# Two transformer blocks on one Trainium2 core: one instruction stream per engine in place of five blocks with barriers, and one modulation product moved to other work units

## The chip, the cores and the metric

The kernel runs on one core of one Trainium2 chip. The metric is the device time of one execution in microseconds, the median over several executions. The core has five engines that run on their own and meet only through semaphores: PE (TensorE, matrix products into the eight PSUM banks), DVE (VectorE), ACT (ScalarE), POOL (GpSimd) and SP (SyncE, which here issues all DMA transfers).

## The reference

Two transformer blocks over one sequence of 256 tokens and 2048 channels, in fp32. Block one: RMS norm, a projection `h @ w_in` whose columns feed a dilated window attention and a gated linear attention, the output projection, then `x + (silu(h @ w_gate) * (h @ w_up)) @ w_down` and a final norm. Block two: a vector c gives six rows of 2048 modulation values,

```
mod = c @ w_ada_2 + b_ada_2          # 2048 x 12288: shift, scale, gate, twice
h = rms_norm(x) * (1 + scale1) + shift1
proj = h @ w_in_2                    # retention, RWKV-7 and block attention
x = x + gate1 * (mixed @ w_out_2)
h = rms_norm(x) * (1 + scale2) + shift2
u = conv3(h @ w_ffn_up_2)            # causal, three taps, per channel
x = x + gate2 * ((silu(u_gate) * u_value) @ w_ffn_down_2)
out = rms_norm(x)
```

## The kernel before

**Weights.** Each large matrix comes in loads of 1 MB (`raw_weights`, four places). A load is two units of 128 x 1024. For each unit ACT writes the high part (`split_hi`, L267), DVE the rest (`split_lo`, L274), and PE makes three products (high x high, high x low, low x high), so that fp32r products give fp32 accuracy. There are four places for split units and the splits run `AHEAD = 3` units ahead: while PE multiplies unit n, ACT and DVE split unit n + 3. `load` lets SP issue load l only when the units that were in its place are split; `split_hi` waits for the load to land and for PE to be done with the unit four before. A unit is 24 matmuls of 256 columns (form "T", the result is transposed) or 12 of 512 columns (form "rows").

**Stages, in order:** first mixer (`FirstMixer`), gate and up (`Glu`, 11 turns of 16 units), down (`Down`, 44 tiles of two units), second mixer (`SecondMixer`, 136 units), up with convolution (`stage_conv_glu`, 11 turns of 16 units), down again, final norm. The first three are one block of instructions (`first_block`); the second mixer, the convolution stage, the second `Down` and the final norm are four more. At the end of a block every engine waits for every other one; between the first two POOL also clears the semaphores (L200, `wait_cleared`).

**What happens at each stage's start.** `Down` first splits four tiles of its activations into high and low (L1720, L1755), which it may do only when the stage before has written them all, in program order; PE begins when `pair_free[0]` and the first low tile are there. The second mixer turns its normalized rows on PE (`turn`, L2050, a matmul with a scaled identity): four of sixteen before the first unit, and two beside each of units 0 to 5. The convolution stage has `Norm`: all sixteen turns first (L402), with L413/L423 and a split of four tiles at a time (L284, L297), then the first unit.

**Modulation.** `mod` is made in twelve groups of 1024 columns. For a group SP issues eight loads of 1 MB (`Ada.load`, L480, two places), DVE makes 16 products (`Ada.product`, L495; the first L497) and PE sums over partitions with 8 matmuls of one column (`Ada.sums`, L507, 16 records in the profile). `Ada.load` m makes SP wait until product 2(m-1) is made, and the weight loads behind it wait too: there is one queue. Groups 6 to 8 are made during `Down` and summed by PE at its end (L1704, 24 matmuls, 48 records). Group 9 belongs to the second mixer: loads at weight loads 57 to 64, products at units 112 to 127, sums at unit 131. Units 104 to 135 are the output projection.

**Second mixer's work beside the units.** `side` (PE), `scalar_side` (ACT) and `vector_side` (DVE) hold what each engine does after unit n. For RWKV, DVE has one instruction or a few in each of units 13 to 35: L2781 at 32 feeds PE's head sums (L2118) at 33, L2789 at 35 feeds PE's transposes (L2247) at 36.

Of the kernel before, what the change touches and what calls it, by code (L numbers as in the profile page):

```python
# [21 lines left out]
ds = bass.ds  # L22
# [95 lines left out]
class Kit:  # L118


    def __init__(self, nc, ctx, ins, at):
# [6 lines left out]
        self.norms = self.turns = 0  # L128
# [8 lines left out]
        self.x_splits = self.act_splits = self.ada_groups = 0  # L137
# [8 lines left out]
        self.w_hi, self.w_lo, self.x_hi, self.x_lo, self.a_hi, self.a_lo = (  # L146
            self.sem(n) for n in ("weights_hi", "weights_lo", "x_hi", "x_lo", "act_hi", "act_lo"))
# [7 lines left out]
        self.gated_norm = [self.sem("gated_norm_" + n) for n in ("mean", "rms", "normed", "turned", "out_dve",  # L155
                                                                 "out_act")]
        self.gated_norms = (0, 0, 0)
        self.row_spread, self.row_copied, self.row_copies = self.sem("row_spread"), self.sem("row_copied"), 0
# [3 lines left out]
        self.square_parts = 1  # L162
# [3 lines left out]
        self.n_scaled = self.sem("norm_scaled")  # L166
        self.n_turned = self.sem("norm_turned")
        self.n_out = [self.sem("norm_out_dve"), self.sem("norm_out_act")]
# [4 lines left out]

    def second_half(self):

        at_h = -(-self.nc.sbuf_base // 32) * 32
        self.hT = self.sb("h_T", [P, KT, S])
        self.x_lo_t = self.at_byte("h_lo_T", at_h, [P, KT, S], R32)
# [17 lines left out]
    def clear_sems(self):  # L196

        self.nc.clear_and_free_semaphores(self.first_sems)
        self.first_sems = []
        self.nc.gpsimd.memset(self.stat[:, 61:62], 0.0).then_inc(self.cleared, 1)  # L200
# [77 lines left out]
def split_x_hi(kit, act, norm):  # L278


    for u in range(4):
        if norm:
            norm.out_act(act, u)
        kit.nc.scalar.activation(kit.x_hi_t[:, 4 * u:4 * u + 4, :], kit.hT[:, 4 * u:4 * u + 4, :], ACT.Copy  # L284
                                 ).then_inc(kit.x_hi, 1)


def split_x_lo(kit, dve, base, norm, wait=None):

    for u in range(4):  # L290
        if norm:
            norm.out_dve(dve, u)
    if wait:
        dve.wait_ge(*wait)
    for u in range(4):
        dve.wait_ge(kit.x_hi, base + u + 1)
        kit.nc.vector.tensor_tensor(kit.x_lo_t[:, 4 * u:4 * u + 4, :], kit.hT[:, 4 * u:4 * u + 4, :],  # L297
                                    kit.x_hi_t[:, 4 * u:4 * u + 4, :].bitcast(F32), ALU.subtract
                                    ).then_inc(kit.x_lo, 1)


def multiply_block(kit, pe, form, j, n0, i, use, xbase, mid=None, spans=None):
# [4 lines left out]
    spans = spans or [(q * P, (q + 1) * P) for q in range(4)]  # L307
    xh, xl = kit.x_hi_t, kit.x_lo_t
    pe.wait_ge(kit.pair_free[j], use + 1 + i)
    for u in range(8):  # L310
        n = n0 + u
        s = n % SPLITS
        if xbase is not None and u % 2 == 0:
            pe.wait_ge(kit.x_lo, xbase + u // 2 + 1)
# [34 lines left out]
def rms_scales(kit, dve, r):  # L349


    nc, stat = kit.nc, kit.stat
    parts = stat[:, 0:16].rearrange("p (t b) -> p t b", t=ST)[:, :, 0:kit.square_parts]
# [11 lines left out]
def rms_root(kit, act, r):  # L365

    bring_root(kit, 32)
# [4 lines left out]
class Norm:  # L372
# [3 lines left out]
    def __init__(self, kit, ctx, wcol, bcol=None, modulated=None):  # L376
        self.kit, self.wcol, self.bcol, self.modulated = kit, wcol, bcol, modulated
        self.r, self.turns = kit.norms, kit.turns
        self.diag = kit.sb(f"norm_diag{kit.turns}", [P, ST, P], ctx)
        kit.norms += 1  # L380
        kit.turns += 1

    def scales(self, dve):
        kit = self.kit
        if self.modulated is not None:
            modulation(kit, self.modulated)
        rms_scales(kit, dve, self.r)
        for t in range(ST):
            kit.nc.vector.tensor_scalar(self.diag[:, t, :], kit.c("ident"), kit.stat[:, 20 + t:21 + t], None, ALU.mult
                                        ).then_inc(kit.n_scaled, 1)  # L390

    def root(self, act):
        rms_root(self.kit, act, self.r)

    def turn(self, pe):
        kit = self.kit
        pe.wait_ge(kit.n_scaled, ST * (self.turns + 1))
        for k in range(KT):
            if k >= 4:
                pe.wait_ge(kit.n_out[k % 2], KT // 2 * self.turns + (k - 4) // 2 + 1)  # L400
            for t in range(ST):
                ins = kit.nc.tensor.matmul(kit.ps[:, 4 + k % 4, t * P:(t + 1) * P], lhsT=kit.x[:, t, k * P:(k + 1) * P],  # L402
                                           rhs=self.diag[:, t, :], start=True, stop=True)
            ins.then_inc(kit.n_turned, 1)

    def out_dve(self, dve, u):

        kit = self.kit
        for k in (4 * u, 4 * u + 2):
            dve.wait_ge(kit.n_turned, KT * self.turns + k + 1)  # L410
            src = kit.ps[:, 4 + k % 4, 0:S]
            if self.bcol:
                ins = kit.nc.vector.tensor_scalar(kit.hT[:, k, :], src, self.wcol(k), self.bcol(k), ALU.mult, ALU.add)  # L413
            else:
                ins = kit.nc.vector.tensor_scalar(kit.hT[:, k, :], src, self.wcol(k), None, ALU.mult)
            ins.then_inc(kit.n_out[0], 1)

    def out_act(self, act, u):

        kit = self.kit  # L420
        for k in (4 * u + 1, 4 * u + 3):
            act.wait_ge(kit.n_turned, KT * self.turns + k + 1)
            kit.nc.scalar.activation(kit.hT[:, k, :], kit.ps[:, 4 + k % 4, 0:S], ACT.Identity, scale=self.wcol(k),  # L423
                                     bias=self.bcol(k) if self.bcol else 0.0).then_inc(kit.n_out[1], 1)
        for half in range(2):
            act.wait_ge(kit.n_out[half], KT // 2 * self.turns + 2 * u + 2)


def stage_final_norm(kit, weight, out):


    nc = kit.nc
    r, done = kit.norms, kit.finals
    kit.norms += 1
    kit.finals += 4
    quarters = [(t, slice(half * D // 2, (half + 1) * D // 2)) for t in range(ST) for half in range(2)]
    with nc.Block() as block:  # L437
        @block.vector
        def _(dve):
            rms_scales(kit, dve, r)  # L440
            dve.wait_ge(kit.loaded, kit.loads_done)
            for t, cols in quarters:
# [1154 lines left out]
class Down:  # L1597
# [115 lines left out]
    def scalar(self, act):  # L1713
# [18 lines left out]
        for k in range(4):  # L1732
            tile(k, 0)
# [1521 lines left out]
```

## Time and profile before

| | us |
|---|---|
| median of 3 executions | 2583.23 |
| their range | 2580.23 to 2594.74 |
| profiled execution, its own time | 2582.93 |
| its span, first to last instruction | 2581.0 |
| PE busy | 2505.3 (97%) |
| DVE busy | 1636.0 (63%) |
| ACT busy | 1144.3 (44%) |

The span is what the rows below divide up; 1.9 us of the execution's own time lie outside it. Times within the trace are counted from the first instruction. "PEclk" is the TensorE clock that was granted in a stretch: 1.00 is 2.4 GHz, 0.5 is 1.2 GHz, and a value between is a mixture of the two in time. A busy PE is not yet PE at full speed.

### The profile page before, as it was taken

To read this page: it belongs to the slowest core of one execution; us is meant where nothing else is said; L and a number is where in the kernel's file an instruction comes from. 1 tells how busy PE (TensorE), PEld (TensorE's weight loads), DVE (VectorE), ACT (ScalarE), POOL (GpSimd) and SP (SyncE) were. 2 spreads that over 40 slices of the span, in tenths; PEclk is the share of its full clock that TensorE was granted. 3 is DMA by queue.
4 is the path that set the end of the run, shared out by engine and by line. 5 is a ranking of instruction groups with operands and counts; after the bars stand their busy time and mean duration, and the time that the engine had idled before them with its cause. 6 is when DMAs were issued, how large, how long until landed. Compare 5 with 4: busy or idle time off the path is not lost. (4 is left out here: it accounts for less than half of the span.)

```text
span 2581.0 us, 41890 instructions
## 1 busy us (share of the span) xinstructions
PE 2505.3 (97%) x17370; PEld 2273.9 (88%) x17370; DVE 1636.0 (63%) x1912; ACT 1144.3 (44%) x1477; POOL 0.3 (0%) x5
## 2 busy tenths in 40 slices
PE   8999999999999999999899999987999999989997
PEld 8888778999999997888898999875999999988886
DVE  4566548777767756777665465556688666654455
ACT  5454344534334334444654333433544444544443
POOL 0000000000000000000000000000000000000000
PEclk9999999999999999999899999998999999999998
DMA  7454457778778767887455334545677555555552
GB/s 268 158 165 157 138 184 273 270 263 292 254 283 279 263 218 261 295 292 273 148 193 162 101 118 130 167 162 212 245 279 276 194 191 190 192 189 184 182 192 98
DMA packets 213832, 541.26 MB, mean 210 GB/s; under 512 B 9050, under 2 KB 14756, under 8 KB 201668
## 3 DMA queue, kind: packets, MB, share of 16 engines
q1 hardware_dynamic: 213700, 539.37, 60.2%
q8 instruction: 99, 1.62, 0.3%
q14 instruction: 33, 0.27, 0.0%
HBM read 534.06 MB, written 5.28 MB: 209 GB/s over the span
## 5 line engine op out<-in xcount | busy, mean ns | idle before, releaser
L274 DVE TENSOR_TENSOR weights_lo<-raw_weights,weights_hi 128x1024 fp32r<-128x1024 f32 x794 | 968.0, 1224 | 830.2 <-ACT weights_hi L267 827.7
L267 ACT ACTIVATE weights_hi<-raw_weights 128x1024 fp32r<-128x1024 f32 x794 | 838.9, 1061 | 1279.0 <-PE ps L334 493.3
L495 DVE SCALAR_TENSOR_TENSOR ada_acc<-ada_w,col,ada_acc 128x1024 f32<-128x1024 f32 x180 | 230.2, 1279 | 2.2 <-DMA ada_w<-in_w_ada_dram 2.1
L334 PE MATMUL ps<-h_hi,weights_hi 128*128 128x256 f32 x1408 | 218.9, 277 | 1.4 <-issue 1.4
L334 PE MATMUL ps<-h_lo_T,weights_hi 128*128 128x256 f32 x1408 | 217.9, 277 | 0.0
L334 PE MATMUL ps<-h_hi,weights_lo 128*128 128x256 f32 x1408 | 217.9, 277 | 0.0
L334 PE MATMUL ps<-glu_x_hi,weights_hi 128*128 128x256 f32 x1280 | 202.8, 280 | 0.0
L334 PE MATMUL ps<-glu_x_lo,weights_hi 128*128 128x256 f32 x1280 | 202.7, 280 | 0.0
L334 PE MATMUL ps<-glu_x_hi,weights_lo 128*128 128x256 f32 x1280 | 202.4, 279 | 0.0
L334 PEld LDWEIGHTS ps<-h_hi,weights_hi 128*128 128x128 f32 x1408 | 186.8, 188 | 2.5 <-issue 2.5
L334 PEld LDWEIGHTS ps<-h_hi,weights_lo 128*128 128x128 f32 x1408 | 186.7, 188 | 0.0
L334 PEld LDWEIGHTS ps<-h_lo_T,weights_hi 128*128 128x128 f32 x1408 | 186.6, 188 | 0.0
L334 PEld LDWEIGHTS ps<-glu_x_hi,weights_hi 128*128 128x128 f32 x1280 | 173.2, 188 | 0.0
L334 PEld LDWEIGHTS ps<-glu_x_lo,weights_hi 128*128 128x128 f32 x1280 | 173.1, 188 | 0.0
L334 PEld LDWEIGHTS ps<-glu_x_hi,weights_lo 128*128 128x128 f32 x1280 | 172.9, 187 | 0.0
L1691 PE MATMUL ps<-weights_hi,h_hi 128*128 128x512 f32 x352 | 112.0, 400 | 7.0 <-DVE h_lo_T L1755 7.0
L1691 PE MATMUL ps<-weights_hi,glu_x_hi 128*128 128x512 f32 x352 | 111.2, 397 | 3.5 <-DVE glu_x_lo L1755 3.5
L1691 PE MATMUL ps<-weights_hi,h_lo_T 128*128 128x512 f32 x352 | 111.6, 398 | 0.0
L1691 PE MATMUL ps<-weights_lo,h_hi 128*128 128x512 f32 x352 | 111.5, 398 | 0.0
L1691 PE MATMUL ps<-weights_hi,glu_x_lo 128*128 128x512 f32 x352 | 111.4, 398 | 0.0
L1691 PE MATMUL ps<-weights_lo,glu_x_hi 128*128 128x512 f32 x352 | 111.2, 397 | 0.0
L1820 PE MATMUL ps<-m_x_hi,weights_hi 128*128 128x256 f32 (+1 forms) x576 | 95.9, 288 | 0.0
(438 smaller groups left out, 3559.4 us busy)
## 6 DMA issues: line engine op xcount, KB each, us to landing
raw_weights<-in_w_in_dram SPq DMA_DIRECT2D x101, 1024.0 KB, 5.2
ada_w<-in_w_ada_dram SPq DMA_DIRECT2D x96, 1024.0 KB, 7.2
raw_weights<-in_w_ffn_up_dram SPq DMA_DIRECT2D x88, 1024.0 KB, 5.2
raw_weights<-in_w_gate_dram SPq DMA_DIRECT2D x44, 1024.0 KB, 5.2
raw_weights<-in_w_up_dram SPq DMA_DIRECT2D x44, 1024.0 KB, 5.3
raw_weights<-in_w_down_dram SPq DMA_DIRECT2D x44, 1024.0 KB, 4.9
raw_weights<-in_w_ffn_down_dram SPq DMA_DIRECT2D x44, 1024.0 KB, 4.8
raw_weights<-in_w_out_dram SPq DMA_DIRECT2D x32, 1024.0 KB, 7.2
```

The source lines that it names most:

```text
L267: kit.nc.scalar.activation(kit.w_hi_t[:, n % SPLITS, :], raw, ACT.Copy).then_inc(kit.w_hi, 1)
L274: kit.nc.vector.tensor_tensor(kit.w_lo_t[:, n % SPLITS, :], raw, kit.w_hi_t[:, n % SPLITS, :].bitcast(F32), ALU.subtract).then_inc(kit.w_l ...
L334: ins = nc.tensor.matmul(out, lhsT=lhsT, rhs=rhs, start=start and m == 0, stop=(k == KT - 1 and m == 2), skip_group_check=True)
L495: step = nc.vector.scalar_tensor_tensor(acc, w, c, acc, ALU.mult, ALU.add)
L1691: ins = nc.tensor.matmul(kit.ps[:, 4 * t + 2 * half + q, :], lhsT=lhsT, rhs=rhs, start=(k == 0 and m == 0), stop=(k + past == w_tiles - 1 ...
L1820: ins = nc.tensor.matmul(out, lhsT=lhsT, rhs=rhs, start=start and m == 0, stop=ends and m == 2, skip_group_check=True)
```

## The change

It rewrites how the stages are put together:

1. All stages are in one block: each engine has one stream from first to last stage. POOL clears the first stages' semaphores while `Down` runs. Semaphores take the place of the barriers: the second mixer's DVE waits for `square_sums >= 8`, SP for `x_weighted >= 4`, the convolution stage for the mixer's `x_squares`, the final norm for `square_sums_2 >= 4`. The table of the square root is brought to ACT before the last squares (`bring_root`) and no longer by `rms_root`.
2. `Down`'s first four tiles are split by the stage before it: `first_hi` and `first_lo` stand in the last turn of `Glu` (after its 16 splits) and of the convolution stage (before the last taps), into places of their own. PE begins with token half 1 (banks 4 to 7) of each half of the columns, and waits for `pair_free` only before token half 0.
3. `ConvGlu` takes the place of `stage_conv_glu` and `Norm`: the class `Turned`, which is the second mixer's way of turning, for both; so four turns before unit 0 and two beside each of units 0 to 5.
4. Group 9 moves: loads at weight loads 11 to 18 (after `s_x2out`), products at units 15 to 37, sums and copy at unit 45 (bank 7). Groups 6 to 8 are summed by PE beside unit 3 of the second mixer, and no longer at the end of `Down`.
5. Smaller moves: the convolution stage's bias row is loaded before its first weights, its products stand at odd units, `Down` waits for `ada_sum` in both places.

```diff
 class Down:
     def tensor(self, pe):
...
-                for t in range(ST):
-                    h, l = (x[:, k % R, t * P:(t + 1) * P] for x in (kit.x_hi_t, kit.x_lo_t))
+                for t in ((1, 0) if begun else range(ST)):
+                    if begun and t == 0:
+                        pe.wait_ge(kit.pair_free[half], self.pairs[half] + 1)
+                    h, l = (x[k % R][:, t * P:(t + 1) * P] for x in (self.hi, self.lo))
...
-        if self.accs:
-            pe.wait_ge(kit.ada_acc, 16 * (self.lead + len(self.accs)))
-            pe.wait_ge(self.s_square, 1)
+    def ada_sums(self, pe):
...
+    def first_hi(self, act):
+        for k in range(4):
+            self.kit.nc.scalar.activation(self.hi[k], self.act_tile(k, 0), ACT.Copy).then_inc(self.kit.a_hi, 1)
+    def first_lo(self, dve):
+        for k in range(4):
+            self.lo_tile(dve, k, 0)
 class Glu:
     def scalar(self, act):
...
+            if half is None:
+                self.down.first_hi(act)
     def vector(self, dve):
...
+            if half is None:
+                self.down.first_lo(dve)
             dve.wait_ge(kit.weights_used, first + 16 + 16 * i)
 class SecondMixer:
+    ADA = (15, 16, 18, 19, 21, 22, 23, 24, 26, 27, 29, 30, 32, 34, 36, 37)
...
-        ada_loads = (57, 58, 59, 60, 61, 62, 63, 64)
+        ada_loads = (11, 12, 13, 14, 15, 16, 17, 18)
...
-                    sp.wait_ge(kit.weights_used, self.first + self.at["out00"].start)
+                    sp.wait_ge(self.s_x2out, 16)
...
+        if n == 3:
+            self.down.ada_sums(pe)
...
-        if n == 131:
-            self.ada.sums(pe, self.lead + 1, 0)
+        if n == self.RET - 1:
+            pe.wait_ge(self.s_ev, 8)
+            self.ada.sums(pe, self.lead + 1, 0, 7)
...
-        s, at = n - 112, None
-        if 0 <= s < 16:
-            self.ada.product(dve, self.lead, 0, s)
+        if n in self.ADA:
+            self.ada.product(dve, self.lead, 0, self.ADA.index(n))
 class ConvGlu:
     def tensor(self, pe):
...
+                for k in range(4):
+                    self.turned.turn(pe, k)
+                for j in range(2):
...
+                        multiply_part(kit, pe, part, first + 8 * j + u, u, self.x_hi, self.x_lo)
+                        if j == 0 and u < 6:
+                            self.turned.turn(pe, 2 * u + 4)
+                            self.turned.turn(pe, 2 * u + 5)
...
+                if isinstance(i, int) and i == self.turns - 1 and j == 1:
+                    self.down.first_lo(dve)
                 for tap in (1, 0):
```

## Rows read from the trace of the kernel before

**Rows 1.** The page: engines' busy time, one product group, one kind of DMA issue

```profile
PE 2505.3 (97%) x17370; PEld 2273.9 (88%) x17370; DVE 1636.0 (63%) x1912; ACT 1144.3 (44%) x1477; POOL 0.3 (0%) x5
...
L495 DVE SCALAR_TENSOR_TENSOR ada_acc<-ada_w,col,ada_acc 128x1024 f32<-128x1024 f32 x180 | 230.2, 1279 | 2.2 <-DMA ada_w<-in_w_ada_dram 2.1
...
raw_weights<-in_w_out_dram SPq DMA_DIRECT2D x32, 1024.0 KB, 7.2
```

**Rows 2.** Waits from 1690 to 1850: who for whom, total us, times, longest

```profile
ACT weights_hi L267 <- DMA raw_weights<-in_w_out_dram: 56.0, 6, 10.4
...
PE ps L1820 <- DVE weights_lo L274: 19.0, 5, 4.6
...
SPq L480 <- DVE ada_acc L495: 78.5, 6, 25.4
```

**Rows 3.** Windows: stretch, its us, busy us (x instructions) by engine, PEclk, DMA share, GB/s

```profile
979.00:987.00 8.00, 4.45 (x13) 3.49 (x13) 5.11 (x7) 2.29 (x5) 0.00 (x0) 0.79 0.22 58
1000.00:1050.00 50.00, 50.00 (x216) 40.26 (x216) 36.09 (x38) 21.63 (x27) 0.00 (x0) 1.00 0.80 292
1230.90:1248.00 17.10, 9.72 (x48) 9.66 (x48) 12.79 (x18) 9.56 (x18) 0.10 (x1) 0.65 0.06 14
1248.00:1274.30 26.30, 26.30 (x208) 26.12 (x209) 16.91 (x30) 16.29 (x28) 0.00 (x0) 0.90 0.54 177
1307.00:1377.00 70.00, 70.00 (x612) 68.73 (x611) 46.69 (x56) 38.10 (x50) 0.00 (x0) 1.00 0.55 172
1342.00:1370.00 28.00, 28.00 (x238) 27.04 (x238) 21.79 (x25) 11.37 (x14) 0.00 (x0) 1.00 0.62 195
1719.92:1785.00 65.08, 44.01 (x147) 33.71 (x147) 39.30 (x34) 16.58 (x21) 0.00 (x0) 0.82 0.62 222
1804.20:1822.50 18.30, 10.27 (x65) 9.88 (x64) 9.17 (x19) 10.65 (x19) 0.00 (x0) 0.81 0.46 173
2308.30:2321.60 13.30, 6.25 (x17) 4.80 (x16) 7.25 (x15) 4.72 (x10) 0.00 (x0) 0.62 0.46 174
```

**Rows 4.** Timeline of DVE before each `Down`: start, us, instruction

```profile
977.37 1.23 DVE L274 TENSOR_TENSOR weights_lo<-raw_weights,weights_hi 128x1024 fp32r<-128x1024 f32 x1 [1.60 <-ACT weights_hi L267]
...
2312.95 0.06 DVE L3105 MEMSET stat<- 128x1 f32 x1
```

**Rows 5.** Timeline where the two norms before a turn begin, and a sum of one group

```profile
1243.74 0.19 ACT L1746 ACTIVATION_READ_ACCUMULATOR y_squares<-x_weighted 128x1 f32 x1
...
1246.14 0.16 DVE L2654 TENSOR_REDUCE stat<-stat 128x4 f32<-128x8 f32 x1 [3.40 <-POOL stat L200]
...
1808.06 0.19 ACT L2637 ACTIVATION_READ_ACCUMULATOR m_squares<-x_rows 128x1 f32 x1
...
1810.88 10.29 PE L402 MATMUL ps<-norm_diag,x_rows 128*128 128x128 f32 x64 [6.67 <-DVE norm_diag L389]
...
565.70 1.84 PE L507 MATMUL ps<-cst,ada_acc 128*128 128x1 f32 x16
```

**Rows 6.** Timeline of DVE and PE in units 27 to 36 of the second mixer

```profile
1345.11 1.23 DVE L274 TENSOR_TENSOR weights_lo<-raw_weights,weights_hi 128x1024 fp32r<-128x1024 f32 x1 [1.50 <-ACT weights_hi L267]
...
1359.92 1.14 DVE L2781 TENSOR_SCALAR rw_gp<-rw_gp,col 128x256 f32<-128x256 f32 x4
...
1368.59 1.23 DVE L274 TENSOR_TENSOR weights_lo<-raw_weights,weights_hi 128x1024 fp32r<-128x1024 f32 x1 [2.09 <-ACT weights_hi L267]
1369.73 1.22 DVE L2789 TENSOR_TENSOR rw_bonus<-ps,rw_v 128x1024 f32<-128x1024 f32 x1
...
1362.80 1.88 PE L2118 MATMUL ps<-rw_gp,cst 128*128 128x512 f32 x4
...
1373.67 0.60 PE L2247 MATMUL ps<-cst,rw_bet 128*128 128x128 f32 x4
```

**Rows 7.** Windows in the convolution stage, before and after its first row sums

```profile
1850.00:1900.00 50.00, 50.00 (x427) 50.00 (x427) 41.31 (x50) 24.64 (x28) 0.00 (x0) 1.00 0.74 267
1950.00:2000.00 50.00, 50.00 (x443) 50.00 (x442) 41.40 (x50) 24.01 (x28) 0.00 (x0) 1.00 0.79 293
```

More of the change, by code:

```diff
@@ L127, in __init__ @@
         self.loads_done = 0
-        self.norms = self.turns = 0
+        self.norms = self.turned = 0
         self.dve_steps = 0
@@ L275, in split_lo, with multiply_block @@
                                 ALU.subtract).then_inc(kit.w_lo, 1)
[L278 to L302, printed above, removed]
+def multiply_block(kit, pe, x, form, j, n0, i, use, mid=None):
     nc = kit.nc
-    spans = spans or [(q * P, (q + 1) * P) for q in range(4)]
-    xh, xl = kit.x_hi_t, kit.x_lo_t
+    spans = [(q * P, (q + 1) * P) for q in range(4)]
+    xh, xl = x
     pe.wait_ge(kit.pair_free[j], use + 1 + i)
@@ L365, in rms_root @@
 def rms_root(kit, act, r):
-    bring_root(kit, 32)
     act.wait_ge(kit.n_mean, r + 1)
     kit.nc.scalar.activation(kit.stat[:, 18:20], kit.stat[:, 18:20], ACT.Sqrt).then_inc(kit.n_rms, 1)
[L372 to L387, printed above, removed]
-        for t in range(ST):
[L389 to L426, printed above, removed]
@@ L1728, in body @@
                 tile(k + 4, i)
-        if self.after:
-            act.wait_ge(kit.weights_used, first)
-            act.wait_ge(kit.pair_free[1], self.pairs[1] + 1)
-        for k in range(4):
-            tile(k, 0)
         self.in_turns(act, body)
@@ new lines, in row_sums, with sync, body @@
+    def row_sums(self, pe, g):
+        kit, nc = self.kit, self.kit.nc
+        pe.wait_ge(kit.ada_acc, 16 * (self.lead + g + 1))
+        for b in range(2):
+            step = nc.tensor.matmul(kit.ps[:, 4 + 2 * g + b, :], lhsT=kit.c("ones"),
+                                    rhs=self.ada.acc[:, b * UN:(b + 1) * UN], start=True, stop=True)
+        step.then_inc(kit.ada_sum, 1)
+    def sync(self, sp):
+        kit, first, lead = self.kit, self.first, self.lead
+        sp.dma_start(self.gate[:, :], kit.ins["b_ada_2"][:, 2 * UN * lead:2 * UN * (lead + 2)].partition_broadcast(P)
+                     ).then_inc(self.s_gate, 16)
+        def body(i):
+            for m in range(8):
+                if m < 4 or not (isinstance(i, int) and i == self.turns - 1):
+                    col = (0, F2 + UN)[m // 4] + UN * i
+                    load(kit, sp, first // 2 + 4 + m, i, block_src(self.w, m % 4, col))
+                if isinstance(i, int) and i < 4 and m % 2:
+                    if i == 0 and m == 1:
+                        sp.wait_ge(kit.weights_used, first)
+                    self.ada.load(sp, lead + i // 2, 0, 4 * (i % 2) + m // 2)
+        load_block(kit, sp, first // 2, 0, self.w, F2)
+        self.in_turns(sp, body)
+        self.head_next(sp, first // 2 + 8 * self.turns)
@@ new lines, in tensor, with body @@
+    def tensor(self, pe):
+        kit, first, uses = self.kit, self.first, self.uses
+        def body(i):
+            if isinstance(i, int) and i == 0:
+                for k in range(4):
+                    self.turned.turn(pe, k)
+                for j in range(2):
+                    part = Part("T", None, 0, j, 8, ())
+                    pe.wait_ge(kit.pair_free[j], uses[j] + 1)
+                    for u in range(8):
+                        if j == 0:
+                            pe.wait_ge(kit.s_xlo, self.turned.before + 2 * u + 2)
+                        pe.wait_ge(kit.w_lo, first + 8 * j + u + 1)
+                        multiply_part(kit, pe, part, first + 8 * j + u, u, self.x_hi, self.x_lo)
+                        if j == 0 and u < 6:
+                            self.turned.turn(pe, 2 * u + 4)
+                            self.turned.turn(pe, 2 * u + 5)
+                return
+            for j in range(2):
+                mid = None
+                if j == 0 and self.summed(i) is not None:
+                    mid = lambda: self.row_sums(pe, self.summed(i))
+                multiply_block(kit, pe, (self.x_hi, self.x_lo), "T", j, first + 8 * j, i, uses[j], mid)
+        self.in_turns(pe, body)
@@ L3225, in program @@
[L3225 to L3231 removed]
+        base = -(-nc.sbuf_base // 32) * 32
+        t = lambda name, off, shape, dt=F32: kit.at_byte(name, base + off * 1024, shape, dt)
+        tiles = lambda name, off: [t(f"{name}{n}", off + n, [P, S], R32)[:, :] for n in range(4)]
@@ new lines, in wide_head, with head, second_head @@
+        def wide_head(w):
+            def head(sp, l):
+                for k in range(LOADS):
+                    load(kit, sp, l + k, 0, wide_src(w, P * k))
+            return head
+        glu = Glu(kit, first, ada, actT[:, :, :], silu[:, :], ins["w_gate"][0], ins["w_up"][0],
+                  wide_head(ins["w_down"][0]))
+        def second_head(sp, l):
+            for u in range(LOADS):
+                load(kit, sp, l + u, 0, block_src(ins["w_in_2"][0], u, SecondMixer.LOW))
+        lo = [t(f"down_lo{n}", a, [P, S], R32)[:, :] for n, a in enumerate((104, 105, 110, 111))]
```

645 lines of the change are left out of this document (300 added, 345 removed).

## The prediction

> **What bounds the kernel now.** I read the page first: PE is busy for 97% of the span, DVE for 63%, ACT for 44% [rows 1]. So only time in which PE stands still, or runs at the lower clock level, can be won, and any PE work that moves from a gap into a busy stretch costs its full length. I then took windows of 50 us over the whole span to find where PE isn't full or PEclk is under 1.00: the start, the seam from `Glu` to `Down`, the seam into the second mixer, the output projection, the seam into the convolution stage, the seam into the second `Down`, and the end. The list of waits names the reasons, and narrow windows price them [rows 2, 3]. The reader should see in each window both the idle time (length less PE busy) and the clock: a gap of 3.55 us at 979 is followed by 1.2 GHz in part of the stretch, so it costs more than its length.
>
> **The output projection holds the largest loss.** From 1719.92 to 1785.00 PE is busy for 44.01 of 65.08 us, at PEclk 0.82 [rows 3]. A matmul of 512 columns takes 50/216 = 0.2315 us at full clock by the `Down` window [rows 3]; spaced by its starts it is 0.233. Of the 147 matmuls 143 are of the projection, worth 33.4 us, and four small ones 0.7. So 34.1 us of work took 65.1: 21.1 us idle and 9.9 us of slowing, together 31.0. Behind it is one chain: SP stood before `Ada.load` for products of group 9, 78.5 us in six waits, the weight loads behind it were issued late, ACT waited 56.0 us for them, DVE for ACT, and PE 19.0 us for DVE [rows 2]; the remaining 2.0 us idle are an attention step behind the same ACT wait.
>
> **The change part by part**, as differences for the path of PE.
>
> *(a) Group 9 leaves the projection: -31.0.* No load there waits for a product any more. What is late next? The projection's 1 MB per two units is 1 MB in 5.6 us, which the DMA engines do easily (292 GB/s in `Down` [rows 3]), and DVE is free for a third of that stretch already with the products in it. I take all of 31.0; the lower bound is 21.1, the idle time alone, if the clock fell for another reason.
>
> *(b) Group 9 in units 15 to 37: +2.0, bounds 0 and 8.* Sixteen products at 1.28 us (the first 0.75) are 20 us [rows 1]. DVE is busy for 46.69 of the 70 us of these units, so 23.3 are free: it just fits [rows 3]. It fits unevenly. I walked the twenty-odd ticks: each split starts when ACT's is done or when DVE's work before it ends, whichever is later. Up to unit 26 every product falls into idle time within two units. From 1342 to 1370 DVE is busy for 21.79 of 28 us [rows 3], and units 26, 27, 29, 30, 32 and 34 add 7.7 us to 6.2 free ones; DVE's split in unit 33 then starts 2.8 us late, and that of unit 35 (1368.59) 1.9 us late. Who waits for DVE? The splits are three units ahead, over 5 us: not they. Of the side work, L2781 in unit 32 now ends at 1361.1 and would end at about 1362.9; PE wants it at 1362.80: 0.2 us [rows 6]. L2789 ends at 1370.95 and may move to 1372.9; PE wants it at 1373.67 [rows 6]: hidden. Then the loads. A held weight load goes out behind its modulation load, and landed after 7.2 us there [rows 1]. The last one, weight load 18, goes out when DVE has made product 11 in unit 30, at 1358.7 by the walk, lands at 1366, and ACT wants it at 1360.3: ACT and DVE then run about 5 us late, PE doesn't need the unit before 1371, but L2789 comes at about 1375.8, which is 2 us after PE asks. That is my 2.0. The upper bound is that a second load (17) hits as well, and that each of the two costs as much as the mean PE idle in the projection, 19.0/5 = 3.8.
>
> The Trainium skill ("DMA: Bandwidth & Descriptors", "Where 436 GB/s comes from") puts the HBM side of a core at about 358 GB/s; with three loads of 1 MB queued at 1358 that would be 8.8 us to the last of them, by that estimate the stall is near 3.5 us and the sum 1.5 us higher.
>
> *(c) The sums of groups 6 to 8 beside unit 3: +5.1.* This speaks against the change. In the window from 1230.90 to 1248.00 PE has 9.72 us of them, while DVE and ACT finish `Down` and PE has nothing else to do [rows 3]: they are hidden today. In units 0 to 5 of the second mixer PE is full, 26.30 of 26.30 us [rows 3], so there nothing hides them. At full clock 16 records are 1.70 us (1.84 with the last one's tail [rows 5]), so 48 are 5.1. Bounds 5.1 and 9.7 (the half clock of today).
>
> *(d) The seam into the second mixer: -2.15.* ACT's last square ends at 1243.93, DVE's reduction starts at 1246.14 [rows 5]: barrier, clearing and release take 2.2 us, and a direct semaphore some 0.05. The chain from that reduction to the first turn, 1.86 us, stays. The clock is low there before and after; when it comes back may shift by some us, worth half of that: bounds -3.7 and -0.6.
>
> *(e) The seam from `Glu` to `Down`: -5.2.* PE idle 8.00 - 4.45 = 3.55, and 0.21 x 2 x 8.00 = 3.4 us at 1.2 GHz, half of it lost, 1.7 [rows 3]. After the change, DVE's last split ends at 978.6 [rows 4], the four low tiles take 1.4, and the first is there when PE's last product ends at 979.0. PE then has three groups of six matmuls, 4.2 us, before it needs `pair_free[1]`, which comes at about 982.5: hidden, with 0.7 us to spare. Bounds 3.5 and 5.2.
>
> *(f) The seam into the second `Down`: -9.4.* From 2308.30 to 2321.60 PE is idle for 13.30 - 6.25 = 7.05 us, and all that it does there runs at 1.2 GHz (0.38 x 2 x 13.3 = 10.1 us low), 2.8 to 3.0 us lost [rows 3]. Afterwards the tiles are split in what is ACT's idle time before its last taps, and PE has 4.2 us of products. `pair_free[1]` comes at 2313.01 as before [rows 4], which is 0.5 us after PE asks. 7.05 + 2.85 - 0.5 = 9.4. Bounds 6.5 and 9.9.
>
> *(g) The seam into the convolution stage: -2.6.* Today 18.30 us from PE's last product to the first unit [rows 3], and six units of 24 x 50/427 = 2.81 us [rows 7]: 35.2. Then: ACT's squares end at 1808.25 [rows 5]; reduction, root (its table is there now) and scaled identity take 1.4 us (1.86 at the other seam), so the turn starts at 1809.7 where it was 1810.88; the second mixer's six units with their turns last 26.30 us from there [rows 3], here 0.5 more since its first units have narrower tiles, and 0.3 more of low clock. 5.5 + 26.3 + 0.8 = 32.6. Bounds -1 and -6 (below).
>
> *(h) The end: -0.3,* the barrier before the final norm. *(i)* At no cost: the sums of group 9 move from unit 131 to 45, both on a busy PE; the bias row is one more megabyte where DMA is half idle; products at odd units stay in the same stage.
>
> Sum: -31.0 + 2.0 + 5.1 - 2.15 - 5.2 - 9.4 - 2.6 - 0.3 = -43.55. Against the profiled execution's own 2582.93 us that gives 2539.4; the median of the runs, 2583.23, is 0.3 higher. I say **2539 us**.
>
> **The rivals.**
>
> *R1, slower: DVE is late in every unit and the clock falls with it.* With 1.0 to 1.3 us more in 16 units, PE would get short waits throughout units 15 to 37, and go to 1.2 GHz as it does after the waits of 2 to 5 us in the projection (PEclk 0.82). These 70 us of PE work at the low level cost up to 70 us: 2537 + 70 = 2607. It decides from the point at which DVE falls more than about 5 us behind; my walk gives 2.8, about 5 with the late load. The Trainium skill ("TensorE: Matmul & The Clock Gate", "A second HAM failure mode: psum-queue depth-cycling") describes such short waits between groups that let the clock swing. Chance 0.03.
>
> *R2, the queue is held in the new place too.* Six of the eight modulation loads again stand before products; if each made PE wait as in the projection, 31.0 us would come back: 2568. For it: the same queue and the same two places. Against it: here weight loads are asked for seven units ahead, and product pairs are two to four units apart, so that only the last one or two loads are short. Chance 0.07.
>
> *R3, the products of the convolution stage lose their quicker spacing.* It has 427 matmuls in 50 us before its first row sums and 443 after them, at the same clock [rows 7], 117 and 113 ns each. No wait explains it; it depends on what went before. If the new start of the stage leaves it at 117 to the end, 9 turns of 384 matmuls at 4.3 ns more are 15 us: 2554. If it is quick from the start, 3 us are won: 2536. The row sums stay where they were, so I expect no change. Chance of the loss 0.08.
>
> *R4, the early splits don't help:* PE finds another wait at both `Down`s, so (e) and (f) are lost: 2554. Chance 0.07.
>
> **How the numbers follow.** My forecast 0.73, R1 0.03, R2 0.07, R3 0.08, R4 0.07, something unseen 0.02. The forecast's own range is 2532 to 2548 from the bounds of (b), (d), (f), (g). R3 and R4 lie at 2554, so 2531 to 2555 holds over 0.8. A change of 0.5% (13 us) is about what a measurement of this kernel can tell from none: faster 0.96, same 0.015, slower 0.025.
>
> **What the profile after would show.** (a) No ACT wait for `w_out` loads, PEclk 1.00 throughout the projection. (b) DVE over 90% busy from 1340 to 1370, one PE wait of about 2 us near unit 36. (c) 48 records beside unit 3, 5 us, in a PE that is otherwise full. (e, f) No PE gap over 1 us before either `Down`. (g) A gap of 5.5 us. I am wrong if PE waits in units 15 to 37 add up to over 8 us, or if the spacing in the convolution stage is another.

## The result, and the profile after

The kernel after takes 2615.95 us (median of 8 runs, 2603.42 to 2618.50) against 2581.31 us for the kernel before in the same job: ratio 1.0115, 95% interval 1.0085 to 1.0144. It is slower. The profiled execution took 2615.34 us, 76 us above my 2539.

Most of the profile does what the prediction said. These are windows of after, columns as in [rows 3]; the stretches are the seam into the first `Down`, the second mixer's start, units 15 to 37 (two rows), the projection, the convolution stage (six rows) and the second `Down`:

```profile
950.00:1000.00 50.00, 50.00 (x334) 45.69 (x334) 27.66 (x29) 22.50 (x27) 0.10 (x1) 1.00 0.69 245
1250.00:1300.00 50.00, 50.00 (x385) 49.58 (x384) 26.39 (x39) 26.88 (x42) 0.00 (x0) 0.90 0.48 171
1300.00:1350.00 50.00, 50.00 (x431) 49.27 (x431) 39.47 (x46) 28.83 (x39) 0.00 (x0) 1.00 0.70 255
1350.00:1400.00 50.00, 47.38 (x389) 43.93 (x388) 37.07 (x40) 22.04 (x30) 0.00 (x0) 1.00 0.72 248
1700.00:1750.00 50.00, 50.00 (x224) 40.60 (x223) 33.61 (x39) 20.46 (x28) 0.00 (x0) 1.00 0.54 177
1800.00:1850.00 50.00, 46.74 (x376) 46.54 (x375) 32.82 (x45) 25.81 (x35) 0.00 (x0) 0.93 0.56 203
1850.00:1900.00 50.00, 40.50 (x290) 39.48 (x289) 30.37 (x39) 15.44 (x17) 0.00 (x0) 0.87 0.56 199
1900.00:1950.00 50.00, 43.40 (x336) 41.63 (x335) 29.57 (x40) 19.34 (x23) 0.00 (x0) 0.96 0.53 193
1950.00:2000.00 50.00, 40.91 (x303) 40.09 (x303) 25.76 (x30) 14.87 (x17) 0.00 (x0) 0.90 0.62 228
2000.00:2050.00 50.00, 42.39 (x330) 40.62 (x329) 34.21 (x44) 18.98 (x23) 0.00 (x0) 0.97 0.55 195
2050.00:2100.00 50.00, 50.00 (x427) 50.00 (x426) 29.20 (x39) 23.37 (x27) 0.00 (x0) 1.00 0.53 186
2350.00:2400.00 50.00, 49.77 (x216) 39.78 (x215) 29.36 (x40) 23.48 (x32) 0.00 (x0) 1.00 0.53 185
```

The reader is to see: PEclk 1.00 at both `Down`s and in the projection, with no gap but one of 0.2 us in the second `Down`, where [rows 3] have gaps. PE turns the convolution stage's first tiles at 1783.70 us, where before did at 1810.88 [rows 5]: 27 us ahead. Then, from 1800 to 2050, PE has 290 to 376 matmuls in 50 us, where before has 427 [rows 7]. The waits of after from 1810 to 2060, PE's and then DVE's (who for whom, total us, times, longest):

```profile
PE ps L295 <- DVE weights_lo L261: 28.5, 15, 3.9
PE ps L2960 <- DVE ada_acc L395: 4.3, 2, 2.6
PE ps L468 <- DVE weights_lo L261: 3.3, 1, 3.3
```

```profile
DVE ada_acc L395 <- DMA ada_w<-in_w_ada_dram: 85.2, 14, 6.6
DVE ada_acc L397 <- DMA ada_w<-in_w_ada_dram: 6.8, 1, 6.8
```

Before, DVE waited 2.1 us for such loads in the whole program [rows 1]. Now each of this stage's is waited for. The chain of work that ended last in this stretch of after (start, us, what; SP's issue of 0.4 us and pauses under 0.05 us are left out) closes on itself:

```profile
1855.51 6.98 DMA ada_w<-in_w_ada_dram
1862.52 1.28 DVE ada_acc L395
1863.80 2.27 DVE weights_lo L261 x2
1866.07 1.20 DVE ada_acc L395
1867.27 1.15 DVE weights_lo L261
...
1868.84 7.17 DMA ada_w<-in_w_ada_dram
```

A load takes 7 us; the product waits for it; the splits queue behind the product on DVE; and SP issues the next load only when the third of those splits is done, since it stands behind the weight load that waits for that split. One round is 1868.84 - 1855.51 = 13.3 us for four units, which PE does in 4 x 2.81 = 11.2. With DVE's work on the taps between rounds, the 13 intervals from the load at 1823.73 to the last at 2023.1 take 199.4 us, 15.3 each. So, as an estimate, 16 loads take 16 x (15.3 - 11.2) = 66 us more than PE's work, less the three units (8.4 us) by which the splits run ahead: 57 us. Before, such a load was issued four units ahead and was there in time. These rows of before are of SP (SPq) and DVE, a load and the first product that needs it, 8.0 us later:

```profile
1851.58 0.51 SPq L480 DMA_DIRECT2D ada_w<-in_w_ada_dram  x1
...
1859.53 1.28 DVE L495 SCALAR_TENSOR_TENSOR ada_acc<-ada_w,col,ada_acc 128x1024 f32<-128x1024 f32 x1
```

The Trainium skill ("DMA: Bandwidth & Descriptors", "Where 436 GB/s comes from") puts the HBM side at about 358 GB/s. By that estimate the 2.1 MB of a weight load and the modulation load 0.4 us behind it would have landed 5.5 us after the second was issued. The trace has 7.0, and it decides; and one stretch of 10 us (e3, 1860 to 1870) moved 398 GB/s, above that figure.

### The profile page after: what moved, and what is told of

Read it like the earlier page. It is cut to its first block, busy times and chain, and to the rows that moved or that the text cites. A ratio compares the mean times of both kernels' runs of the same rounds, so it can differ in the third digit from the quotient of the medians.

```text
span 2613.6 us, 41798 instructions
## 1 busy us (share of the span) xinstructions
PE 2526.0 (97%) x17370; PEld 2295.8 (88%) x17370; DVE 1634.7 (63%) x1924; ACT 1148.1 (44%) x1488; POOL 0.3 (0%) x5
## 4 chain that ended last, share of the span: by engine, by line
PE 88%; DVE 6%; DMA 4%; issue 1%; ACT 1%; SPq 0%; DVEq 0%; ACTq 0%
PE ps L295 30%; PE ps L1598 18%; PE ps L468 16%; PE ps L1783 14%; DMA ada_w<-in_w_ada_dram 4%; DVE weights_lo L261 2%; DVE ada_acc L395 2%; PE ps L2267 1%; PE ps L2252 1%; PE ps L838 1%; PE ps L1731 1%; PE ps L862 1%; DVE conv_y L3079 1%; PE ps L2264 1%; PE ps L407 0%
## 5 line engine op out<-in xcount | busy, mean ns | idle before, releaser
L295 PE MATMUL ps<-conv_x_hi,weights_hi 128*128 128x256 f32 x1280 | 210.2, 287 | 28.5 <-DVE weights_lo L261 28.5
L295 PEld LDWEIGHTS ps<-conv_x_hi,weights_hi 128*128 128x128 f32 x1280 | 178.7, 193 | 32.5 <-DVE weights_lo L261 31.6
L295 PE MATMUL ps<-conv_x_hi,weights_lo 128*128 128x256 f32 x1280 | 207.1, 284 | 0.0
L295 PE MATMUL ps<-conv_x_lo,weights_hi 128*128 128x256 f32 x1280 | 206.8, 284 | 0.0
L295 PEld LDWEIGHTS ps<-conv_x_hi,weights_lo 128*128 128x128 f32 x1280 | 177.8, 193 | 0.0
L295 PEld LDWEIGHTS ps<-conv_x_lo,weights_hi 128*128 128x128 f32 x1280 | 177.4, 192 | 0.0
L1598 PE MATMUL ps<-weights_hi,down_hi 128*128 128x512 f32 x384 | 121.0, 396 | 0.2 <-DVE stat L3083 0.2
L1598 PE MATMUL ps<-weights_lo,down_hi 128*128 128x512 f32 x384 | 120.7, 396 | 0.0
L1598 PE MATMUL ps<-weights_hi,down_lo 128*128 128x512 f32 x384 | 120.7, 395 | 0.0
L1783 PE MATMUL ps<-m_x_lo,weights_hi 128*128 128x256 f32 (+1 forms) x576 | 91.5, 281 | 0.0
```

Source lines behind the costliest of these rows:

```text
L295: ins = nc.tensor.matmul(out, lhsT=lhsT, rhs=rhs, start=start and m == 0, stop=(k == KT - 1 and m == 2), skip_group_check=True)
L1598: ins = nc.tensor.matmul(kit.ps[:, 4 * t + 2 * half + q, :], lhsT=lhsT, rhs=rhs, start=(k == 0 and m == 0), stop=(k + past == w_tiles - 1 ...
L1783: ins = nc.tensor.matmul(out, lhsT=lhsT, rhs=rhs, start=start and m == 0, stop=ends and m == 2, skip_group_check=True)
```

## The experiments

All times are in us. Each run stands beside the kernel before in its own job. One thing has to be known first, because it moves a run by 15 us whatever the kernel: the 128x256 products of the convolution stage have the two spacings of [rows 7], and **which one an execution gets is not fixed by the kernel**. Of 13 runs of before beside e1 to e4 seven took 2576.9 to 2582.3 and six 2594.6 to 2596.9; the profiled before has 443 in 50 us behind its first row sums, the profiled after 427 to the end. I call them executions *at 113 ns* and *at 117 ns* by the level that the time falls in, checked by windows for the profiled ones, and compare like with like: after is 2603.5 at 113 (2 runs) and 2614 to 2618.5 at 117 (6 runs), before about 2580 and 2596. The change costs 21 to 24 us at equal spacing.

**e1: the modulation loads ahead of the weight load of each even m again, in after.** The expectation calls this four units ahead, as in before. By the trace it is five, since the products stay at odd units: behind the split that releases the load issued at 1845.38 come five more splits before its product at 1854.10.

```diff
+ if isinstance(i, int) and i < 4 and m % 2 == 0 and (i, m) != (0, 0):
+     self.ada.load(sp, lead + i // 2, 0, 4 * (i % 2) + m // 2)
  load(kit, sp, first // 2 + 4 + m, i, block_src(...))
- if isinstance(i, int) and i < 4 and m % 2:
-     if i == 0 and m == 1: sp.wait_ge(kit.weights_used, first)
-     self.ada.load(sp, lead + i // 2, 0, 4 * (i % 2) + m // 2)
+ if isinstance(i, int) and (i, m) == (0, 0):
+     sp.wait_ge(self.mixer.s_xsq, 4 * ST)
+     self.ada.load(sp, lead, 0, 0)
```

> The kernel after, with one thing changed: in the conv stage's first four turns the modulation load of each even m is issued ahead of the weight load (the very first one behind it), instead of behind the weight load of the odd m. That is 4 units ahead of the product that needs it, instead of 1. Theory A (the load reaches its product too late): the 85 us that the DVE's products wait for the load go, and with them the PE's 28.5 + 3.3 us for weight splits and 4.3 us before the row sums, and about 15 us of the 37 us in which the clock was at 1.2 GHz between 1830 and 2050 us: about 51 us less than after, 2565 us (2558 to 2575). Rival B (the products at odd units make the DVE late by their own time): the load wait goes, but the splits stay late; no less than 2600 us. Rival C (the lower clock is the cause and the waits follow it): no change, 2616 us.

Measured: 2545.89 (2542.81 to 2558.74, 4 runs), ratio to before 0.9854 (0.9802 to 0.9906). At 113 ns 2544.7 against 2603.5, at 117 ns 2558.7 (one run) against 2616.9: **58 to 59 us**, and no PE or DVE wait for these loads is left. Its windows, PE alone (PE busy, PEclk, DMA share, GB/s):

```profile
1800.00:1850.00 50.00, 50.00 (x428) 1.00 0.64 235
1850.00:1900.00 50.00, 50.00 (x420) 1.00 0.77 285
1900.00:1950.00 50.00, 50.00 (x443) 1.00 0.79 295
```

From the first turn to the last product the stage takes 494.7 (1783.1 to 2277.8) instead of 566.7 (1783.7 to 2350.4). Of these 72.0, nine turns of 384 products at 4.23 ns are 14.6, the spacing of that one profile; 57.4 are the loads, as the round above gives. My 51 were too few: 36.1 of waits, and 37 us at 1.2 GHz (the PEclk column of after from 1800 to 2050) worth at most 18.5; some 3 us of it I can't place. Theories B and C fall: the products stand at the same odd units, and the clock stays up once the loads are early.

**e2: this part alone in before** (load behind the weight load at odd m, products at odd units). **e12: its other half alone**, products at odd units and loads left where they were.

```diff
- if isinstance(i, int) and i < 4 and m % 2 == 0:      # e2 only
-     ada.load(sp, lead + i // 2, 0, 4 * (i % 2) + m // 2)
  load(kit, sp, first // 2 + 4 + m, i, block_src(w, m % 4, col))
+ if isinstance(i, int) and i < 4 and m % 2:           # e2 only
+     ada.load(sp, lead + i // 2, 0, 4 * (i % 2) + m // 2)
...
- if isinstance(i, int) and i < 4 and u % 2 == 0:      # e2 and e12
+ if isinstance(i, int) and i < 4 and u % 2:
      ada.product(dve, lead + i // 2, 0, 8 * (i % 2) + 4 * j + u // 2)
```

> The kernel before, with only this part of the change: in the conv stage the modulation load is issued behind the weight load of each odd m instead of ahead of that of each even m, and the products move from even to odd units. Theory A: this part alone makes the kernel before slower by what it costs after, 45 to 51 us: 2581 + 48 = 2629 us. Rival B/C (the loss needs the seams without barriers, the turns spread over the units, or the lower clock that comes with them): within 5 us of 2581.

> The kernel before with the conv stage's modulation products moved from even to odd units and the loads left ahead of the weight loads: the other half of the part that made the kernel before 78 us slower. Theory A: the parity of the units costs nothing (2577 to 2597 us as before), and all of the 78 us are the loads' place. Rival: the odd units, with the taps' work behind unit 7, cost the DVE something of their own: over 2600 us.

Measured: e2 2660.49 (2658.77 to 2661.25, 4 runs), ratio 1.0281 (1.0234 to 1.0329); the profiled one is at 117 ns once its modulation loads are over (427 in 50 us at 2200), so it stands 64 us above before at that spacing, more than the 45 to 51 expected: PE waits 40.9 us for splits there, where after has 31.8. Its DVE waits from 1760 to 2060 are much those of after:

```profile
DVE ada_acc L495 <- DMA ada_w<-in_w_ada_dram: 85.4, 13, 7.8
DVE ada_acc L497 <- DMA ada_w<-in_w_ada_dram: 14.1, 2, 7.8
```

e12 is 2588.14 (10 runs: five at 2576.3 to 2581.8, five at 2594.5 to 2596.9), ratio 1.0015 (0.9985 to 1.0045). So the odd units are free, and the loads' place is what costs, with or without the rest of the change.

**e9 and e11: the distance.** e9 keeps the late loads and puts the products one unit later, 2 units behind the issue. e11 keeps the products and puts each load ahead of the odd m's weight load: 3 units.

```diff
- if isinstance(i, int) and i < 4 and u % 2:           # e9
-     self.ada.product(dve, lead + i // 2, 0, 8 * (i % 2) + 4 * j + u // 2)
+ slot = 16 * i + 8 * j + u - 2 if isinstance(i, int) else -1
+ if 0 <= slot < 64 and slot % 2 == 0:
+     self.ada.product(dve, lead + slot // 32, 0, slot // 2 % 16)
```

> The kernel after with its late modulation loads (still behind the weight load of each odd m), and the conv stage's modulation products one unit later: at even units again, so 2 units behind their load's issue instead of 1. Theory A (what costs is the distance from issue to product, since a load lands some 7 us after it is issued and a unit takes 2.8 us): the DVE still waits, about 3 us a load instead of 6 (45 us in all instead of 93), but its splits run 3 units ahead of the PE and take that in: PE waits for splits of 0 to 8 us instead of 32, and 2546 to 2565 us. Rival Q (two loads issued back to back share the queue, so that weights and modulation rows both land late whatever the distance): the PE keeps 25 us or more of its waits, over 2595 us.

> The kernel after with its products where they are (odd units), and each modulation load issued ahead of the odd m's weight load instead of behind it: 3 units ahead of its product, where after has 1, the run with later products 2 and the one with early loads 4. The issue follows the DVE's own progress (it waits for a split), so a late DVE issues late: theory A' is that the distance counts in the DVE's work once it is behind (splits of 1.2 us and products of 1.3 us, so 2 units are some 4 us against 7.1 us to land, which gave the 4 us that the run with later products still waited for each load), and in the PE's 2.8 us units while it is not. With 3 units that is 8.4 us against 7.1 us: on time from the start and then always, so 2546 us (2543 to 2560), no DVE wait over 1 us for a load. Rival: 3 units are not enough, because the DVE is behind at the stage's start; then 1 to 2 us a load and 2565 to 2590 us.

Measured: e9 2597.52 (10 runs: one at 2583.8, nine at 2596.6 to 2601.5), ratio 1.0051 (1.0027 to 1.0075); e11 2553.17 (2543.6, 2547.6, 2558.7, 2558.9), 0.9862 (0.9808 to 0.9917). The waits of PE in e9 (1810 to 2060), then of DVE in e11 (1780 to 2060):

```profile
PE ps L2960 <- DVE ada_acc L395: 19.0, 2, 9.6
PE ps L295 <- DVE weights_lo L261: 13.0, 10, 1.9
```

```profile
DVE ada_acc L395 <- DMA ada_w<-in_w_ada_dram: 10.4, 7, 2.8
```

At equal spacing (117 ns) one unit of distance costs 58 us, two 39, three (e11) and five (e1) nothing; before has four. e11's time is as expected, but its DVE still has waits of up to 2.8 us, where I said none over 1. e9 missed theory A. It met rival Q's numbers (over 2595 us, and 32.0 us of PE waits), yet not by Q's reason that the distance doesn't matter: DVE's waits for the loads go from 92.0 us with one unit to 53.5 with two and 10.4 with three. In theory A I had taken the splits' lead for a reserve that swallows each wait, but in a closed round it is spent once. By the rows of the chain a round with two units is 7.1 + 1.28 + 2.27 = 10.7 us and with three 7.1 + 1.28 + 1.15 = 9.5; four rounds and DVE's 7.9 us for taps and result (2 x 3.21 + 1.22 + 0.25) are 50.5 and 46.0 a turn, against PE's 45.0. So three units just keep pace (e11: DVE still waits 10.4 us, PE never), and two fall behind by 5.5 us a turn, 22 in four turns; less the 8.4 us of lead that is 14, and PE's waits for splits are 13.0. The larger part of e9's 39 is another: the last product of each group now comes a unit later, which puts it behind the taps and the result of the turn, and the row sums wait 19.0 us for it. PEclk of 0.90 to 0.96 in three windows of 50 us is worth at most 10 us more.

**e3: the 48 sums in the gap ahead of the turn** (on e1).

```diff
- if n == 3: self.down.ada_sums(pe)
...
+ pe.wait_ge(self.squares_in, 1)
+ self.down.ada_sums(pe)
  for k in range(4): self.turned.turn(pe, k)
```

> The kernel with the early loads, and the 48 ones-products for modulation groups 6 to 8 taken from behind unit 3 of the second mixer and put ahead of its first turn, where the PE waits 15 us for the diagonal anyway. Theory: the 7.45 us that they took behind unit 3 go, and the 10.2 us at 1.2 GHz that followed them go too (about 4 to 5 us): 11 to 12 us under the run with the early loads. Rival: the clock falls at that place because of the 15 us wait ahead of the first turn and not because of the sums; then only 7 us, or, as the engine is busier in that wait, 7 us plus what the clock gives back in units 0 and 1.

Measured: 2534.38 (2532.6 to 2535.4 three times, 2548.37), ratio 0.981 (0.9757 to 0.9864): 11 us under e1 by the medians, 9.4 by the profiles (last product on `down_hi` at 2514.5 against 2523.9), where 11 to 12 were expected. The sums of after, with the window of PE around them, and those of e3:

```profile
1259.28 7.45 PE L1613 MATMUL ps<-cst,ada_acc 128*128 128x1 f32 x48
```

```profile
1259.28:1266.70 7.42, 7.42 (x51) 0.71 0.43 144
```

```profile
1229.52 10.37 PE L1613 MATMUL ps<-cst,ada_acc 128*128 128x1 f32 x48 [4.54 <-ACT ps L1662]
1240.11 3.78 PE L1731 MATMUL ps<-m_diag,x_weighted 128*128 128x128 f32 x16 [0.22 <-DVE m_diag L1720]
```

In the gap they run at PEclk 0.50 and take longer, and the turn still begins at 1240.1 (1240.36 in after). In after the clock fell under them: 0.71 x 7.42 = 5.3 us at full clock, the prediction's 5.1. The window 1250 to 1300 is at 1.00 in e3, at 0.90 in after: the low clock there went with the sums. But e3 also fills most of the 15 us gap ahead of the turn, so it can't tell whether the sums alone make the clock fall, or the sums so soon behind that gap.

**e4: group 9 back beside the projection** (on e1): `ADA = tuple(range(112, 128))`, its loads at 57 to 64, its sums behind unit 131.

> The kernel with the early loads, and modulation group 9 put back where it was before: its loads at weight loads 57 to 64 and its products at units 112 to 127, beside the projection. My sum priced the move at -31.0 us in the projection and +2.0 us in units 15 to 37. If that holds, this run is 29 us slower than the one with the early loads (26 to 31). Rival: most of the projection's loss was something else that the change removed (the barrier and the turns behind it); then 0 to 10 us slower.

Measured: 2572.76 (10 runs: seven at 2568.7 to 2575.4, three at 2585.4 to 2587.0), ratio 0.9951 (0.9920 to 0.9981). Medians at 113 ns: 2570.2 - 2544.7 = 25.5 us slower than e1; at 117 ns 2585.9 - 2558.7 = 27. PE waits for splits again (20.6 us in 5, as the 19.0 of [rows 2]). The move is worth a little under my 29, and the first of the two figures lies just outside the 26 to 31 expected.

**e7: the first four tiles split at `Down`'s own start** (on e1): `first_hi` and `first_lo` move from the stage ahead into `Down.scalar` and `Down.vector`, behind a wait for that stage's last result.

> The kernel with the early loads, and the first four tiles of each Down stage split at the Down's own start (behind the last product of the stage ahead) instead of ahead. It undoes the early splits alone and keeps the single program without barriers. My sum gave the two Down seams -14.6 us together, waits and clock, by the early splits and the missing barrier in one. If the early splits carry it, this run is 8 to 15 us slower than the one with early loads, with PE waits of 3 to 6 us for down_lo or down_hi at each seam and a stretch at 1.2 GHz behind them. Rival (the missing barrier carries it, and the splits are quick enough at the seam): 0 to 4 us slower.

Measured: 2571.10 (10 runs: three at 2556.7 to 2558.0, seven at 2570.4 to 2573.1), ratio 0.993 (0.9902 to 0.9959). At equal spacing 12 to 13 us slower than e1, in the 8 to 15 expected. The two waits, from 900 to 1300 and from 2200 to 2500:

```profile
PE ps L1594 <- DVE down_lo L1629: 3.5, 1, 3.5
```

```profile
PE ps L1594 <- DVE down_lo L1629: 6.7, 1, 6.7
```

These are nearly the gaps of before (3.55 and 7.05). The early splits carry the two seams. No run takes away the barrier alone; what the predicted 14.6 leaves for it is some 2 us, an estimate.

**e8, e5, e6, e10: the spacing** (all on e3).

```diff
- rhs=self.ada.acc[:, b * UN:(b + 1) * UN]             # e8: one column each
+ rhs=self.ada.acc[:, b * UN:b * UN + 1]
...
+ mid = lambda: [nc.tensor.matmul(kit.ps[:, 7, :], lhsT=kit.c("ones"), rhs=kit.x[:, 0, b * UN:(b + 1) * UN], ...)
+                for b in range(2)]   # e5: Glu turn 1; e6: conv turn 1; e10: as e6, banks 4 and 5
```

> The kernel with the sums in the turn wait, and each 128x512 product of the conv stage's row sums cut to one column. This leaves out most of the second feed-forward's gate: 511 of each 512 of its row sums are not formed. Theory S: without the 128x512 f32 products the spacing stays at 117 ns in all executions, as it does in all runs through the Glu stage, whose own modulation sums are one column wide: 2548 us each time, none at 2533. Rival (another event of the third turn switches it): executions at 2533 as before.

> The kernel with early loads and the sums in the turn wait, and two more 128x512 products of ones with f32 rows (results unused) behind the first unit of the Glu stage's turn 1. In every run so far the small products of a stage of the conv's kind are 117 ns apart, and in some executions 113 ns from the first pair of row sums on (443 instead of 427 records in 50 us). Theory S (a pair of 128x512 f32 products in the stream can switch the spacing, wherever it stands): the Glu stage of this run goes at 443 from turn 1 on in some executions, which gives back up to 430 us x 4/117 = 15 us there against 1.3 us that the pair takes: 2520 us where it switches, 2536 where it does not. Rival P (the spacing belongs to the conv stage, its tiles or its code): the Glu stage stays at 427, 2536 us.

> The same kernel as the one with the sums in the turn wait, and one more pair of such products in turn 1 of the conv stage, a turn ahead of the first real pair. Theory S: the spacing may switch a turn earlier, 23 us x 4/117 = 0.8 us less against 1.3 us more, so the time is the same within 1 us where it switches, and executions that do not switch are rarer. Rival P: the switch stays at the first real pair in turn 2.

> The kernel with an extra pair of 128x512 products of ones with f32 rows in the conv stage's turn 1, now written to banks 4 and 5 as the first real pair of row sums is, instead of both to bank 7. With bank 7 that extra pair left the records at 87 in 10 us, and the real pair a turn later moved them to 91. If the banks or two different banks make the switch, 91 from turn 1 on (0.8 us less from there); if not, 87 until turn 2. Either way 2533 to 2536 us where it switches and 2548 where it does not.

Measured: e8 2546.23 (2544.6 to 2549.6, 4 runs), none at 2533, and 427 in 50 us through the whole stage of its profile. e5 2541.73 (2536.0, 2541.5, 2542.0, 2551.2); its profile, the slowest, has 427 in both stages. e6 2533.61 (2532.4 to 2537.9, 4 runs). e10 2534.47 (four at 2532.6 to 2535.3, then 2538.4 and 2542.3). Windows of e6 (ahead of its added pair, behind it, behind the first real pair):

```profile
1810.00:1820.00 10.00, 10.00 (x87) 1.00 0.83 310
1850.00:1860.00 10.00, 10.00 (x87) 1.00 0.44 153
1900.00:1910.00 10.00, 10.00 (x91) 1.00 0.52 187
```

and of e10 (behind the added pair, behind the first real one, behind the second):

```profile
1850.00:1860.00 10.00, 10.00 (x87) 1.00 0.77 290
1950.00:1960.00 10.00, 10.00 (x87) 1.00 0.55 203
1990.00:2000.00 10.00, 10.00 (x91) 1.00 0.37 124
```

In these kernels, where the step comes, it comes at a real pair: the first in e1, e3, e6 and e7, the second in e10, neither in the profiles of after, e4, e5 and e11; the added pairs never brought it in a profile, on bank 7 or on 4 and 5. But a pair isn't the only place, and theory S doesn't hold as I had it. e12's profile has the quicker spacing from its first unit on (1820), 90 us ahead of its first pair (1909.43):

```profile
1850.00:1900.00 50.00, 50.00 (x443) 1.00 0.81 305
```

and e2's goes from one to the other ahead of any pair of its stage. These are its windows on either side of a wait, and the wait:

```profile
1822.00:1832.00 10.00, 10.00 (x90) 1.00 0.57 210
1836.00:1846.00 10.00, 10.00 (x87) 1.00 0.89 316
```

```profile
1835.25 0.74 PE L334 MATMUL ps<-h_hi,weights_hi 128*128 128x256 f32 x4 [1.71 <-DVE weights_lo L274]
```

At 1854.3, when its clock is back from 1.2 GHz, four products take 0.453 us again, 113 ns each. So these changes follow a break in the row of 128x256 products (a pair, a wait, a stretch at the low clock), but not every break brings one. e8 shows only that four of four executions without the full pairs had no step. Why one break brings a change and another doesn't stays open. The times aren't two clean levels either: e10's 2542.3 is more than the 3 us that two turns at 117 ns explain, and e5's 2541.5 and 2542.0 lie between its 2536.0 and 2551.2.

## Why the prediction was wrong, point by point

- **The step that failed is the last clause of (i):** "products at odd units stay in the same stage", put down at no cost. The products are indeed free (e12). What I didn't walk was SP: the same edit moved each load from ahead of one weight load to behind the next, and with it the issue from four units ahead of its product to one (2.8 us, where a load takes 7.0 to land). Measured: 58 us (e1), alone in before 64 us (e2), and nothing at three units (e11). For (b) I followed the loads through the queue one by one; for this stage I looked at DVE alone.
- **R3 came true in the profile, but that the change causes it isn't shown.** It is worth 14.6 us, as worked out there. Before has executions of both kinds too, 23 of its 64 at 117 ns, and its profiled one happened to be at 113. With 6 of 8 runs at 117, the median of after lies 12 us above its quicker runs. Where PE waits ahead of the row sums nearly all runs are at 117 (after 6 of 8, e2 4 of 4, e9 9 of 10), but e7, without that wait, has 7 of 10: whether the wait matters is open.
- **(c)** was +5.1 with bounds to 9.7, and is 9.4 by the profiles, 11 by the medians (e3): at its upper bound or over it. The full-clock work was right, 5.3 us; what was missing is the clock, which fell to 1.2 GHz under the sums and stayed there behind them.
- **(a) and (b)** held together: -29.0 predicted, -25.5 to -27 measured (e4). (b) held in its mechanism too: ACT waits 7.0 us for a held weight load, DVE then 4.2 us for ACT, and PE's one wait in units 15 to 37 is 2.6 us for `rw_bonus`, where I had 2.0. So R2's price of 31 us did not come.
- **(e) and (f)** held: no gap over 0.3 us at either `Down`, and e7 puts 12 to 13 us of the 14.6 down to the early splits. R4 did not come. **(d)** and **(g)** held in the profile: the turns begin at 1240.36 and 1783.70, the second with a gap of 5.5 us.
- **R1's mechanism** showed in another place: waits of up to 3.9 us in the convolution stage, and PEclk 0.87 to 0.97 with them. The Trainium skill ("TensorE: Matmul & The Clock Gate", "A second HAM failure mode: psum-queue depth-cycling") says that short idle times between groups can make the clock swing; the trace agrees, with 37 us at 1.2 GHz between 1800 and 2050.

The profiled execution of after is 72.5 us above that of e1: 57.4 for the loads and 14.6 for its spacing, within 0.5 us. That of e1, 2542.8, is 3.4 above my 2539.4, which is closer than the terms are: (c) cost 4.3 us more by the profiles and (a) and (b) gave 3.5 less, so the other parts gave 4.4 us more than their sum. 0.9 of it is ahead of the second mixer's first turn (at 1239.79 in e1, 1248.00 in before, so -8.2 where (d) and (e) say -7.35). The rest I can't place, and so much of the agreement is luck. The best version is e3, 2534.38 us, which beats before by 1.9% and after by 3.1%, and before by 1.7% at equal spacing (2533.4 against 2577.4).

## What to carry to other kernels

When an edit moves a transfer's place in an issue queue, count the distance from its issue to its consumer in that queue, before and after, and hold it against the landing time of the profile; here 1 unit cost 58 us, 2 units 39, and 3 or more nothing. Where the issue waits for the very engine that waits for the transfer, the delay is a closed round: its length against the bound engine's pace gives the loss, and work done ahead pays for it only once. Look at the spread of the runs for two levels before comparing medians.

## What was not expected of the hardware

- The 128x256 products have two spacings at full clock, 427 and 443 in 50 us, and the same kernel's executions differ by 15 us through it. Most steps came at a pair of 128x512 f32 products, but not at every pair, and two profiles have the quicker spacing ahead of any pair of the stage: e12 from the stage's first unit on, and e2, which left it behind a wait of PE of 1.71 us. What decides it is open.
- 48 products of one column took 7.45 us in the full stream (155 ns each, at PEclk 0.71) and 10.37 us in the gap at the lower clock. In after the clock fell to 1.2 GHz with them although PE was busy throughout (50.00 of 50.00 us at PEclk 0.90).
